# Expert multiplications in plain float32 on column tiles, with 96 slots a job, in a two-layer hybrid encoder

## The reference, cut to what matters

```python
D_MODEL, SEQ, DEPTH, D_FF_EXPERT, N_EXPERTS, TOP_K = 1024, 256, 2, 2816, 8, 2
for l in range(DEPTH):
    x = layer_norm(ALPHA * x + hybrid_mixer(x, ...))       # RG-LRU heads beside windowed attention
    if l % 2 == 0:
        ffn = (silu(x @ wg) * (x @ wu)) @ wd               # dense
    else:
        logits = x @ router_w + router_b
        top_logit, top_idx = top_k(logits, 2)
        top_w = softmax(top_logit)
        ffn = sum over the token's two experts e of top_w * ((silu(x @ wg[e]) * (x @ wu[e])) @ wd[e])
    x = layer_norm(ALPHA * x + ffn)
```

## Time and profile before

| | us |
|---|---|
| median of the runs shown | 1206.38 |
| the profiled execution | 1205.96 |
| its span in the trace | 1204.0 |
| busy in the span: TensorE / VectorE / ScalarE | 1174.8 / 994.2 / 811.1 |
| from the first expert matmul to the last, about | 399 to 1189 |

### The profile page before, as it was taken

One profiled execution on the slowest core, in us unless ns is written; L12 is line 12 of the kernel. 1 busy time (PEld: TensorE's weight loads), 2 busy tenths in 40 slices (PEclk: granted clock), 3 DMA queues, 4 the chain that ended last, 5 costly groups with the idle time before them and its releaser, 6 DMA issues.

```text
span 1204.0 us, 18178 instructions
## 1 busy us (share of the span) xinstructions
PE 1174.8 (98%) x5908; PEld 981.1 (81%) x5908; DVE 994.2 (83%) x1255; ACT 811.1 (67%) x1100; POOL 21.0 (2%) x21
## 2 busy tenths in 40 slices
PE   8998999998999999999999999999999999999996
PEld 8976888887987888888888888888888888888884
DVE  6787545456687898998999898899899899889988
ACT  4774444343585776876876786787687687778765
POOL 0011000001000000000000000000000000000001
PEclk9998999999999999999999999999999999999999
DMA  9844555552523699998999999899899899998930
GB/s 387 335 174 157 194 194 190 194 181 101 207 83 136 256 361 342 351 368 330 360 367 336 354 356 352 336 352 351 343 345 364 343 360 342 361 350 350 360 125 35
DMA packets 48256, 342.69 MB, mean 285 GB/s; under 512 B 5648, under 2 KB 5776, under 8 KB 6880
## 3 DMA queue, kind: packets, MB, share of 16 engines
q1 hardware_dynamic: 46944, 336.11, 73.1%
q0 software_dynamic: 992, 5.56, 1.3%
q10 hardware_dynamic: 288, 0.59, 0.1%
HBM read 341.18 MB, written 1.05 MB: 284 GB/s over the span
## 4 chain that ended last, share of the span: by engine, by line
PE 90%; DVE 5%; ACT 3%; issue 1%; DMA 1%; DVEq 0%; SPq 0%; ACTq 0%
PE bank L420 18%; PE bank L422 18%; PE bank L421 18%; PE bank L572 9%; PE bank L578 9%; PE bank L575 9%; PE bank L647 3%; PE bank L593 2%; PE bank L414 1%; ACT whi L762 1%; ACT scr L866 1%; PE bank L653 1%; PE bank L652 1%; DVE wlo L1006 1%; DMA raw<-W 1%
## 5 line engine op out<-in xcount | busy, mean ns | idle before, releaser
L1368 DVE TENSOR_TENSOR wlo<-raw,whi 128x1024 fp32r<-128x1024 f32 x528 | 616.3, 1220 | 40.3 <-ACT whi L967 39.9
L967 ACT ACTIVATE whi<-raw 128x1024 fp32r<-128x1024 f32 x528 | 520.5, 1052 | 0.0
L420 PE MATMUL bank<-whi,ah 128*128 128x512 f32 (+1 forms) x976 | 382.5, 392 | 3.6 <-DVE al L1018 3.0
L422 PE MATMUL bank<-whi,al 128*128 128x512 f32 (+1 forms) x976 | 372.9, 382 | 0.0
L421 PE MATMUL bank<-wlo,ah 128*128 128x512 f32 (+1 forms) x976 | 372.7, 382 | 0.0
L420 PEld LDWEIGHTS bank<-whi,ah 128*128 128x128 f32 x976 | 185.9, 190 | 36.1 <-DVE al L1018 3.7
L422 PEld LDWEIGHTS bank<-whi,al 128*128 128x128 f32 x976 | 185.6, 190 | 35.5
L421 PEld LDWEIGHTS bank<-wlo,ah 128*128 128x128 f32 x976 | 186.2, 191 | 31.6
L1006 DVE TENSOR_TENSOR wlo<-raw,whi 128x1024 fp32r<-128x1024 f32 x110 | 130.4, 1222 | 28.1 <-ACT whi L762 27.1
L762 ACT ACTIVATE whi<-raw 128x1024 fp32r<-128x1024 f32 x114 | 115.3, 1057 | 22.3 <-PE bank L422 17.2
L572 PE MATMUL bank<-whi,hth 128*128 128x512 f32 x400 | 125.0, 394 | 0.3
(11 more groups left out here) (232 smaller groups left out, 1036.9 us busy)
## 6 DMA issues: line engine op xcount, KB each, us to landing
raw<-W SPq DMA_DIRECT2D x319, 1024.0 KB, 5.1
scr<-gb_d POOLq DMA_DIRECT2D x3, 1024.0 KB, 5.0
scr<-wbd_d POOLq DMA_DIRECT2D x2, 512.0 KB, 6.2
x<-gb_d POOLq DMA_DIRECT2D x1, 1024.0 KB, 4.9
out_d<-acc SPq DMA_DIRECT2D x4, 256.0 KB, 2.0
x<-x_d SPq DMA_DIRECT2D x1, 512.0 KB, 3.8
x<-x_d ACTq DMA_DIRECT2D x1, 512.0 KB, 7.9
rtab<-rt_d POOLq DMA_DIRECT2D x1, 228.0 KB, 2.8
```

Source lines behind the costliest of these rows:

```text
L420: nc.tensor.matmul(out, sh, mh, start=first, stop=False, skip_group_check=True)
L422: return nc.tensor.matmul(out, sl, mh, start=False, stop=last, skip_group_check=True)
L967: nc.scalar.activation(whi[:, q % SPLIT, h * HW:(h + 1) * HW], raw[:, q % RING, h * HW:(h + 1) * HW], ACT.Copy).then_inc(hi_rdy, 1)
L1368: V.tensor_tensor(wlo[:, q % SPLIT, h * HW:(h + 1) * HW], raw[:, q % RING, h * HW:(h + 1) * HW], whi[:, q % SPLIT, h * HW:(h + 1) * HW].bi ...
```

## The change

In the expert phase no weight and no activation is split any more. TensorE multiplies plain float32 straight from `raw`. A job has 96 slots instead of 128 (`CAP`), and there are 8, 16 or 24 jobs, by whether the fullest expert has over 96 or over 192 rows. The slots fall in two groups with matmuls of their own:

- `low_slots`: slots 0 to 63 as a stationary operand of 64 columns. Two blocks of 512 columns of weights are multiplied on the two 64-column halves of the array. A piece has four such matmuls.
- `high_slots`: slots 64 to 95 as an operand of 32 columns, and four blocks of 256 columns on the four 32-column quarters. A piece has eight such matmuls. In the two gate and up pieces of the eleventh chunk they lie on two of the quarters only, with twice the matmuls on each.

Even pieces do low then high, odd ones high then low. A piece of gate and up now holds two chunks of 256 columns for a quarter of the contraction (`experts` lays it out so), but for the two pieces of the eleventh chunk; still 33 pieces an expert. h is worked out for two chunks at once, on 128 partitions for low and 128 for high, by two instructions instead of one each on ScalarE and VectorE (`silu`, `make_h`), and turned by three transposes a pair. `gather` multiplies plain `x` and `S` (16 plain float32 matmuls of 96 columns), `scatter` keeps its two parts and fp32r but reads 96 partitions and comes one matmul pair at a time, after four different pieces. TensorE's result for the down weights lies over both halves or all four quarters of a bank, so copying it out (`yh`, `yl`) takes six instructions instead of one on each of the two engines. The slot of `raw` is freed by TensorE's last matmul on it (`freed`), and SyncE waits for that. Ahead of the phase the two split copies of `x` (L788, L1025) and the splitting of the experts' first pieces are gone; behind it `y32` is copied out by ScalarE and VectorE side by side.

```diff
+CAP = 96
+LOW = 64
+NP = NCH // 2
+XORDER = [("G", 0, r) for r in range(4)]
+for _p in range(1, NP + 1):
+    XORDER += [("G", _p, r) for r in range(4 if _p < NP else 2)]
+    XORDER += [("D", _p - 1, cc) for cc in range(2)]
+XORDER += [("D", NP, 0)]
...
+SCAT_AFTER = {XLAST["G", 0]: (0, 0), XORDER.index(("G", 1, 1)): (0, 1), XLAST["G", 1]: (1, 0),
...
+                        sp.wait_ge(freed, r * RING + (s + 2 - RING))
...
+                    for t in range(NT):
+                        last = nc.tensor.matmul(bank[:, GB[b], k * P:k * P + CAP], x[:, t, kk * P:(kk + 1) * P],
+                                                S[:, t, :], start=(t == 0), stop=(t == NT - 1))
...
+            def scatter(t, n):
+                nc.tensor.matmul(bank[:, 4, :], ST[0:CAP, t, :], yh[0:CAP, n * 512:(n + 1) * 512], start=True, stop=False)
...
+            def low_slots(kind, p, r, slot):
+
+                w = raw[:, slot, :]
+                b = xfree(p)[0]
+                if kind == "D":
+                    for j in range(2):
+                        for n in range(2):
+                            last = nc.tensor.matmul(bank[n * LOW:(n + 1) * LOW, 2, :], h_low(p, r, j),
+                                                    w[:, j * D + n * 512:j * D + (n + 1) * 512],
+                                                    start=p == 0 and r == 0 and j == 0,
+                                                    stop=p == NP and j == 1, skip_group_check=True)
+                elif p < NP:
+                    for k in range(2):
+                        kk = 2 * r + k
+                        for cc in range(2):
+                            last = nc.tensor.matmul(bank[cc * LOW:(cc + 1) * LOW, b, :], xg[:, kk, 0:LOW],
+                                                    start=kk == 0, stop=kk == KT - 1, skip_group_check=True)
...
+            def high_slots(kind, p, r, slot):
+
+                w = raw[:, slot, :]
+                m = CAP - LOW
+                b = xfree(p)[1]
+                if kind == "D":
+                    for j in range(2):
+                        for q in range(4):
+                            last = nc.tensor.matmul(bank[q * m:(q + 1) * m, 3, 0:256], h_high(p, r, j),
+                                                    w[:, j * D + q * 256:j * D + (q + 1) * 256],
+                                                    start=p == 0 and r == 0 and j == 0,
+                                                    stop=p == NP and j == 1, skip_group_check=True)
+                else:
+                    for k in range(2 if p < NP else 4):
+                        kk = (2 if p < NP else 4) * r + k
+                        for q in range(4 if p < NP else 2):
+                            at = (2 * k + q // 2) * 512 if p < NP else k * 512
+                            gu = w[:, at:at + 512].rearrange("p (a n) -> p a n", a=2)
+                            last = nc.tensor.matmul(bank[q * m:(q + 1) * m, b, 0:FC].rearrange("p (a n) -> p a n", a=2),
+                                                    xg[:, kk, LOW:CAP], gu[:, :, (q % 2) * P:(q % 2 + 1) * P],
+                                                    start=kk == 0, stop=kk == KT - 1, skip_group_check=True)
+                return last
+            def turn_pair(p):
+                if p < NP:
+                    for k in range(3):
+                        last = nc.tensor.transpose(bank[:, 6, k * P:(k + 1) * P], he[:, k * P:(k + 1) * P], ident[:])
...
-                for i, (kind, c) in enumerate(FFORDER):
-                    slot = (STREAM + i) % SPLIT
-                    for h in range(2):
-                        pe.wait_ge(lo_rdy, j * (2 * FFP) + (2 * (STREAM + i) + h + 1))
...
-                            last = downmm(slot, h, (hth[:, c % 2, h * P:(h + 1) * P], htl[:, c % 2, h * P:(h + 1) * P]),
...
-                            for k in (2 * h, 2 * h + 1):
-                                last = gate_up(slot, "AB".index(kind), k, xgh, xgl, 0, c % 2)
-                        last.then_inc(used, 1)
...
+                for i, (kind, p, r) in enumerate(XORDER):
+                    slot = i % RING
+                    pe.wait_ge(raw_in[slot], j * (16 * FFP // RING) + 16 * (STREAM // RING + i // RING + 1))
+                    if kind == "G" and p == 0 and r == 0:
+                        pe.wait_ge(xg_sb, 2 * j + 2)
+                    if kind == "D" and r == 0:
+                        pe.wait_ge(hT_sb, j * (NP + 1) + (p + 1))
+                    if i % 2 == 0:
+                        low_slots(kind, p, r, slot)
+                        high_slots(kind, p, r, slot).then_inc(freed, 1)
+                    else:
+                        high_slots(kind, p, r, slot)
+                        low_slots(kind, p, r, slot).then_inc(freed, 1)
+                    if i in XT_AFTER:
+                        q = XT_AFTER[i]
+                        pe.wait_ge(h_rdy, j * (NP + 1) + (NT * NCH + q + 1))
+                        turn_pair(q)
...
-                        scatter(t, 0, 4)
-                        scatter(t, 1, 5)
+                            pe.wait_ge(acc_rdy, j * 4 + (2 * t + n))
...
+                            pe.wait_ge(st_sb, j + 2)
+                            pe.wait_ge(S_rdy, j + 2)
+                        gather(b)
...
+                def silu(p):
+                    lo, up_ = xfree(p)
+                    act.wait_ge(freed, j * FFP + (XLAST["G", p] + 2))
+                    n = FC if p < NP else P
+                    m = P if p < NP else LOW
+                    nc.scalar.activation(he[:, 0:n], bank[:, lo, 0:n], ACT.Silu)
+                    nc.scalar.activation(he[0:m, FC:FC + P], bank[0:m, up_, 0:P], ACT.Silu).then_inc(silu_rdy, 1)
...
+                        nc.scalar.activation(hT[:, p % 2, :], bank[:, 6, 0:FC + P], ACT.Copy).then_inc(hT_sb, 1)
...
+                for n in range(2):
+                    nc.scalar.activation(yh[0:LOW, n * 512:(n + 1) * 512], bank[n * LOW:(n + 1) * LOW, 2, :], ACT.Copy)
+                for q in range(4):
+                    last = nc.scalar.activation(yh[LOW:CAP, q * 256:(q + 1) * 256], bank[q * m:(q + 1) * m, 3, 0:256],
+                                                ACT.Copy)
+                last.then_inc(yh_sb, 1)
...
-                        nc.scalar.activation(whi[:, q % SPLIT, h * HW:(h + 1) * HW],
-                                             raw[:, q % RING, h * HW:(h + 1) * HW], ACT.Copy).then_inc(hi_rdy, 1)
...
-                        V.tensor_tensor(wlo[:, q % SPLIT, h * HW:(h + 1) * HW], raw[:, q % RING, h * HW:(h + 1) * HW],
-                                        whi[:, q % SPLIT, h * HW:(h + 1) * HW].bitcast(F32),
-                                        ALU.subtract).then_inc(lo_rdy, 1)
...
+                    V.tensor_tensor(he[:, 0:n], he[:, 0:n], bank[:, lo, n:2 * n], ALU.mult)
+                    V.tensor_tensor(he[0:m, FC:FC + P], he[0:m, FC:FC + P], bank[0:m, up_, P:2 * P],
+                                    ALU.mult).then_inc(h_rdy, 1)
...
+                V.tensor_copy(xg[:, 4:8], bank[:, GB[1], :].rearrange("p (k s) -> p k s", k=4)[:, :, 0:CAP]
+                              ).then_inc(xg_sb, 1)
```

More of the change, by code:

```diff
@@ L413, in keep_warm @@
                 for _ in range(n):
-                    nc.tensor.matmul(bank[:, b, :], src[:, 0:P], src, start=True, stop=True)
+                    last = nc.tensor.matmul(bank[:, b, :], src[:, 0:P], src, start=True, stop=True)
+                return last
             def split_ready(ph, t, g):
@@ L683, in router @@
                                  stop=True).then_inc(pos_ps, 1)
-                keep_warm(WARM["slots"], 4)
+                keep_warm(WARM["slots"], 4).then_inc(freed, 1)
             mixer(0)
@@ L958, in _ @@
+                last.then_inc(yh_sb, 1)
+                silu(0)
+                turned(0)
+                for p in range(1, NP + 1):
+                    silu(p)
+                    if p == NP:
+                        rows(j + 1)
+                    turned(p)
+                    if p == 2:
                         act.wait_ge(st_ps, j + 1)
-                        nc.scalar.activation(ST[:], bank[:, 7, 0:2 * P].rearrange("p (t n) -> p t n", t=NT),
+                        nc.scalar.activation(ST[0:CAP], bank[0:CAP, 4, 0:2 * P].rearrange("p (t n) -> p t n", t=NT),
@@ L973, in _ @@
-            act.wait_ge(used, njob * (2 * FFP) + 2 * STREAM)
-            for n in range(2):
-                nc.scalar.activation(y32[:, n * 512:(n + 1) * 512], bank[:, 2 + n, :], ACT.Copy).then_inc(yh_last, 1)
+            act.wait_ge(freed, njob * FFP + 1)
+            nc.scalar.activation(y32[0:LOW, 0:512], bank[0:LOW, 2, :], ACT.Copy)
+            for q in range(2):
+                last = nc.scalar.activation(y32[LOW:CAP, q * 256:(q + 1) * 256],
+                                            bank[q * (CAP - LOW):(q + 1) * (CAP - LOW), 3, 0:256], ACT.Copy)
@@ L977, in _ @@
+            last.then_inc(yh_last, 1)
```

(8 more changed lines are left out.)

330 lines of the change are left out of this document (157 added, 173 removed).

## The result

| | before | after |
|---|---|---|
| device time, median | 1205.77 us (1204.35 to 1206.52, 4 runs) | 1287.88 us (1286.51 to 1289.11, 4 runs) |
| ratio, 95% interval | 1 | 1.068 (1.066 to 1.070) |
| span of the profiled execution | 1204.0 us | 1284.7 us |
| one job of the expert phase | 98.7 us | 109.7 us |

The account below looks back on a forecast made before the run. TensorE's instruction stream was taken as the bound: streams of 94.4 us plus tile changes of 9.2 made 103.6 us a job against 98.7, so 1206.0 + 8 x 4.9 + 1.3 gave 1246 us, 3.3% slower; range 1182 to 1310 us.

Parts of the forecast that it names:

- What bounds it, and that splitting lies beside it: Expert phase: TensorE's own instruction stream sets 98.7 us a job; splitting on ScalarE and VectorE is hidden under it.
- Streams, 94.4 us a job: TensorE's matmuls and transposes in a job after the change, without changes of tile: 94.4 us.
- rival 3: High groups: four quarters don't run at once; 1461 us, milder forms from 1300 us; chance 0.14 for all.
- the prediction's estimate of 1311 us: High groups at the Trainium skill's factors for tiles: 1.12 us each, total time about 1311 us.
- Changes of tile, 9.2 us a job: TensorE in a job: 34 width changes at 0.14 us (4.8) and 13 whole-array excursions at 0.20 + 0.14 (4.4).
- Rivals 1 and 2: Tile changes nearly free, 1173 to 1190 us, chance 0.25; only width changes free, 1208 us, chance 0.06.
- rival 4: Dearer tile changes, 0.20 to 0.25 us each: 106.4 to 109.4 us a job, 1269 to 1293 us; chance 0.08.
- Waits for DMA and h: Expert phase: weight loading and h stay covered by TensorE's work, so TensorE waits for neither.
- Start and end, 1.3 us: Outside the jobs' sum: 0.6 us lost copying rows at the start, 0.7 on copies before the last scatter.
- The sum, "8 x 4.9 + 1.3": Whole kernel: eight jobs each 4.9 us longer, plus 1.3 at start and end, added to 1206.0 us: 1246.5.
- The upper part of the range: Total time above the forecast's own 1230 to 1264 us, up to 1310, taking in rival 4 and mildest rival 3.

Follow-up runs that it names:

- Experiment 6: Kernel after the change, with every piece done low then high instead of alternating: 1310.23 us, 1.086 of the kernel before.
- Experiment 1: Kernel after the change, with TensorE's loop over the jobs written out eight times (no pass for fuller experts): 1242.59 us, 1.030 of the kernel before.
- 2: Kernel before the change, with each expert matmul of 512 columns issued as two of 256, in all 33 pieces: 1283.07 us, 1.062 of the kernel before.
- 3: Kernel before the change, with matmuls of 512 columns issued as two of 256 in only the first 18 pieces, then 24: 1223.32 us and 1254.55 us.
- 4: Kernel after the change, with two jobs written out in the body of TensorE's loop, which then runs four times: 1261.92 us.
- 5: Control: kernel before the change, with only TensorE's job loop written out eight times: 1206.2 us, 1.0005 of the kernel before.

## Why the prediction was right or wrong

- *What bounds it, and that splitting lies beside it*: right. TensorE's stream carries the phase before and after; 627 us less of busy VectorE in the phase bought nothing.
- *Streams, 94.4 us a job*: right. Low starts come 0.43 us apart with both tiles at it, and a high group of 16 needs no more than its 0.86 and a change; rival 3 (four quarters not at once, 0.14) is out. The page of the Trainium skill that stood beside it, "TensorE: Matmul & The Clock Gate" (Measured speedup vs the span model), gives 3.07 times for four row tiles, from which the prediction's estimate of 1311 us came, and 2.38 for three column tiles; the four column tiles of plain float32 here come to the full factor, 0.86 us for 16 streams of 0.216.
- *Changes of tile, 9.2 us a job*: right. Two equations from the jobs written out, if the streams are the forecast's 94.4 us in both: 34x + 13y = 103.4 - 94.4 and 2x + 6y = 96.7 - 94.4, so x = 0.14 us for a change between 64 and 32 wide and y = 0.34 for an excursion to the whole array. The forecast had 0.14 and 0.20 + 0.14. Experiment 6 gives 0.147 for x by itself. Rivals 1 and 2 needed less than 0.07, or nothing, for each, and are out, and so is rival 4. The rule of the Trainium skill ("TensorEngine Tiling (Array Packing)", Key Properties), that a change of tiling mode drains TensorE, agrees with the 0.14 us for a change of width; that the time goes into a drain no run here shows.
- *Waits for DMA and h*: right, none of either in the phase.
- *Start and end, 1.3 us*: 0.5 in the net. Written out, 38.1 us more in the span are 8 x 4.7 and 0.5. The end alone cost what was forecast for it: TensorE's wait for the last copy is 1.6 us, where it was 0.8.
- **The sum, "8 x 4.9 + 1.3", is the step that failed.** It takes the loop's boundary as free in both kernels, as it is in the kernel before. The sum counted what every instruction costs and never how many there are. A piece has 12 written matmuls in both kernels, but each plain float32 one is two instructions with a load each: a piece went from 12 matmuls with 12 loads to 24 with 24, the loop's body from 1030 records to 1760, and between 1462 and 1610 it stops staying with TensorE. Each of the seven jumps then costs 6.1 us (42.6 / 7): 4.4 standing still, 1.7 nearly all from the half clock. Why the standstill lasts 4.4 us, where a transfer of the instruction queue takes about 1, stays open. Experiment 1 takes it away (and leaves the forecast's own figure: 1242.6 us against 1246), 2 puts it into a kernel without tiles, 3 finds the size, 4 shows that it is paid by the jump, 5 that nothing else comes of writing out a loop. It wasn't among the rivals either; rival 4's 106 to 109 us a job looked near, for another reason. The upper part of the range was there for rivals 3 and 4, both of which are out, so that 1287.9 lies in it is luck. The direction isn't: without the jump's price the kernel is still 36 us slower, for the reason given.

I could have seen it. The page of before shows 21 transfers on the instruction queue for a program with eight passes through 1030 instructions, so the loop was being kept; and that a float32 matmul is two streams was in my own sum, so the new body's length could be worked out. The Trainium skill ("Advanced Engine Details and Errata", ISA Cache) gives 128 KB for TensorE in lines of 16 KB, 256 instructions each. The traces agree on the line: 87 fetches are 1.43 MB, 16 KB each, and 758 records more in the loop (704 to 1462) cost 3 fetches more. By that figure eight lines hold 2048 instructions; the loop of 1760 was fetched again on each pass all the same, so the whole of it doesn't count as room for a loop. That section says nothing of a jump's price.

## What to carry to other kernels

Count the instructions of an engine's loop body, not only their times: when a change doubles them, look at the instruction queue's transfers and at "issue" waits right behind the jump, and write the loop out if its body no longer stays (here somewhere between 1460 and 1760 instructions of TensorE, with every second jump paying at 1610). A stall has a second price, since TensorE comes back at half clock. When work is cut into tiles of different widths, sort it by width: at 0.14 us a change and 0.34 an excursion the order of the same matmuls was worth 6.7 us of 103.

## What the runs showed of the hardware that I had not expected

- A TensorE loop of 1030 or 1462 instructions passes its jump without a gap; at about 1610 every second jump costs some 6 us; at 1760 and 1822 each one does (6.1 us in both). A straight run of nearly 14,000 instructions shows no wait for its code (TensorE idles 1.6 us in 832).
- Behind a standstill of 4.4 us TensorE's granted clock was 0.58 over the next five us, and behind two shorter ones close together 0.50 over six; then 1.00 again.
- Four column tiles, 32 wide, in plain float32 run truly at once (16 streams of 256 columns in 0.86 us and a change).
- One core's loads ran at 414 GB/s over 641 us with all DMA engines busy.
